# Four chained pairs of Strassen block products in place of eight plain up tiles, with sixteen modulation dots moved ahead of them

## The reference, cut to what matters

```python
h = modulate(rmsnorm(x, norm2_g[l]), sh2, sc2)
x = x + g2[:, None, :] * (jnp.square(jax.nn.relu(h @ w_up[l])) @ w_down[l])
shf, scf = jnp.split(c_act @ w_ada_final + b_ada_final, 2, axis=-1)
return modulate(rmsnorm(x, final_g), shf, scf)
```

## Time and profile before

| | us |
|---|---|
| median of 3 runs | 1181.98 |
| lowest, highest | 1180.6, 1182.74 |
| the profiled execution | 1180.96 |
| its span, first to last instruction | 1179.3 |
| PE busy | 1143.8 |
| DVE busy | 778.9 |
| ACT busy | 413.6 |

### The profile page before, as it was taken

The page is one execution under the profiler, slowest core; times in us unless marked ns, Lnnn a source line. Parts: engine busy times, 40 slices in busy tenths (PEclk is TensorE's granted clock), DMA queues, the critical chain, the costliest instruction groups (busy, mean ns, idle before and its releaser), DMA issues.

```text
span 1179.3 us, 17099 instructions
## 1 busy us (share of the span) xinstructions
PE 1143.8 (97%) x6522; PEld 1061.9 (90%) x6522; DVE 778.9 (66%) x1342; ACT 413.6 (35%) x683; POOL 76.9 (7%) x111
## 2 busy tenths in 40 slices
PE   6899999999999999999999999999999999999997
PEld 3786678888999999999889999999999999999886
DVE  6667898777645754565536677685756666457884
ACT  5521134454621211332316422253443525123324
POOL 3001110000111210000000000000000000000000
PEclk9899999999999999999999999999999999999998
DMA  9924553222252222275222241212221224223533
GB/s 354 361 71 161 168 203 131 80 74 71 82 179 99 98 99 98 97 278 160 91 72 108 90 138 58 71 58 68 72 67 59 72 73 142 72 89 117 166 91 108
DMA packets 45315, 139.96 MB, mean 119 GB/s; under 512 B 4876, under 2 KB 10588, under 8 KB 44093
## 3 DMA queue, kind: packets, MB, share of 16 engines
q1 hardware_dynamic: 28848, 81.36, 20.8%
q0 software_dynamic: 11344, 44.83, 11.0%
q10 hardware_dynamic: 5052, 12.81, 3.2%
HBM read 123.25 MB, written 15.74 MB: 118 GB/s over the span
## 4 chain that ended last, share of the span: by engine, by line
PE 92%; DVE 4%; issue 1%; ACT 1%; DMA 1%; SPq 0%; DVEq 0%; ACTq 0%
PE acc_ps L677 44%; PE acc_ps L1124 11%; PE acc_ps L755 11%; PE wk L1103 10%; PE wk L976 3%; PE wk L802 2%; PE wk L954 2%; PE acc_ps L762 1%; PE wk L895 1%; PE wk L916 1%; PE wk L905 1%; PE wk L795 1%; DMA xT_in<-in_x_T 1%; PE wk L868 0%; PE wk L929 0%
## 5 line engine op out<-in xcount | busy, mean ns | idle before, releaser
L677 PE MATMUL acc_ps<-act_hilo,w_hi 128*128 128x384 f32 x1792 | 398.1, 343 | 6.1 <-DVE act_hilo L1633 3.0
L677 PEld LDWEIGHTS acc_ps<-act_hilo,w_hi 128*128 128x128 f32 x1792 | 317.8, 190 | 26.6 <-issue 23.5
L677 PE MATMUL acc_ps<-act_hilo,w_lo 128*128 128x384 f32 x896 | 229.2, 336 | 0.0
L677 PEld LDWEIGHTS acc_ps<-act_hilo,w_lo 128*128 128x128 f32 x896 | 163.5, 190 | 0.0
L1587 DVE TENSOR_TENSOR w_lo<-w_raw,w_hi 128x1024 fp32r<-128x1024 f32 x70 | 85.5, 1222 | 91.9 <-ACT w_hi L1172 90.9
L1124 PE MATMUL acc_ps<-hid_st,w_st_hilo 128*128 128x384 f32 x768 | 134.3, 335 | 0.0
L1124 PEld LDWEIGHTS acc_ps<-hid_st,w_st_hilo 128*128 128x128 f32 x768 | 133.0, 188 | 0.7 <-issue 0.7
L1172 ACT ACTIVATE w_hi<-w_raw 128x1024 fp32r<-128x1024 f32 x70 | 73.7, 1053 | 95.3 <-PE acc_ps L677 87.9
L2116 DVE SCALAR_TENSOR_TENSOR xT<-acc_ps,modT,xT 128x384 f32<-128x384 f32 (+2 forms) x96 | 40.6, 479 | 58.9 <-PE acc_ps L1124 58.9
L2031 DVE CUSTOM_DVE_ANT_0 dot_out<-dot_ring,c_rows 128x1024 f32<-128x1024 f32 x48 | 58.8, 1224 | 5.1 <-DVE hidden_hilo L2047 4.3
L1678 DVE CUSTOM_DVE_ANT_0 dot_out<-dot_ring,c_rows,vecT 128x1024 f32<-128x1024 f32 x48 | 61.5, 1281 | 0.9
(11 more groups left out here) (259 smaller groups left out, 1861.6 us busy)
## 6 DMA issues: line engine op xcount, KB each, us to landing
w_raw<-in_w_pre SPq DMA_DIRECT2D x50, 512.0 KB, 3.5
dot_ring<-in_w_ada_cols POOLq DMA_DIRECT2D x48, 512.0 KB, 3.9
w_raw<-in_w_up SPq DMA_DIRECT2D x32, 512.0 KB, 3.5
w_raw<-in_w_down SPq DMA_DIRECT2D x16, 512.0 KB, 4.0
w_raw<-in_w_down_half SPq DMA_DIRECT2D x32, 256.0 KB, 2.6
spec<-filt_out POOLq DMA_DIRECT2D x12, 512.0 KB, 3.2
gate_spill<-gates_out ACTq DMA_DIRECT2D x16, 384.0 KB, 2.3
hy_spec<-spec SPq DMA_DIRECT2D x12, 512.0 KB, 5.5
```

The lines of the kernel that those rows point to most:

```text
L677: mm = pe.matmul(acc_ps[:, slot, 512 * h:512 * h + HALF], w[:, kw, :], src[:, x, k, HALF * h:HALF * h + HALF], start=(first and i == 0), s ...
```

## The change

- `NCH` and the second plain `up` go. The eight up tiles behind the groups become pairs 8 to 11 (`NPAIR` is 12), one behind another with no down tiles between them. Pairs 8, 9 and 10 use on ACT and DVE the list of an even pair (now a function `pair_ahead`), which prepares the next pair's operands; pair 11 ends with the splits of the first two tiles of the last down part among its own steps. The last down part reads its eight hidden blocks with the last two exchanged (0 to 5, 7, 6).
- Sixteen of the 24 late dots move from `up(1)` and the last down part into the four groups, four in each: behind combine 1 of the odd pair, behind the first down low part of the odd pair, and behind the residuals of down tiles 1 and 3. They use one row buffer, `ring3`, in place of two: POOL loads the next row when both sums of the dot before are done.
- The three late weight operands of a pair lie in a part of the activations that is free by then; the hidden blocks lie in `hid`; the sum of operand 6 shares its buffer with that of operand 1. Nothing else of the arithmetic changes.

The diff, cut to its core:

```diff
-            up_weights(1, first=1)
-            down_weights(1)
+            for q in range(2 * NHC, NPAIR):
+                pair_weights(q)
+            for m in range(KD):
+                if m < 2:
+                    pair_used(NPAIR - 1, m)
+                else:
+                    sp.wait_ge(hi_done, T_MLP + 16 + m - 1)
+                    sp.wait_ge(lo_done, T_MLP + 16 + m - 1)
+                sp.dma_start(raw[m % 2][:], w_down[KD + m]).then_inc(landed[m % 2], 16)
...
-            pool.wait_ge(st_mm, 7 * 2 * NHC)
-            pool.dma_start(cb2[:]...).then_inc(ld_c, 16)
-            late_loads(KD, DOTS - DOTS_OUT)
+            pool.wait_ge(acc_ready, A_MLP + 16)
+            pool.dma_start(cb3[:]...).then_inc(ld_c, 16)
+            for n in range(KD, DOTS - DOTS_OUT):
+                pool.wait_ge(dot_done, 2 * DOTS_OUT + 2 * n)
+                pool.dma_start(ring3[:], w_adaT[n + DOTS_OUT]).then_inc(ld_dot[2], 16)
...
-            pe.wait_ge(sd_free, KD * NHC)
-            up(NCH - 1)
+            for q in range(2 * NHC, NPAIR):
+                for j in range(7):
+                    product(q, j)
...
+            def spare_dot(n):
+
+                if n == KD:
+                    dve.wait_ge(ld_c, 48)
+                dve.wait_ge(ld_dot[2], 16 * len([i for i in range(DOTS_OUT) if i % 3 == 2]) + 16 * (n - KD + 1))
+                dve.wait_ge(late_done, n + 1)
+                for g in range(2):
+                    dve.wait_ge(dot_done, 2 * DOTS_OUT + g + 2 * n)
+                    dve.tensor_tensor_reduce(junk3[:], ring3[:], cb3[:, g], 1.0, 0.0, ALU.mult, ALU.add,
+                                             dacc[:, g:g + 1]).then_inc(dot_done, 1)
+                dve.wait_ge(dot_done, 2 * DOTS_OUT + 2 + 2 * n)
+                mt = n + DOT0 + DOTS_OUT
+                dve.tensor_scalar(modT[:, mt, :], dacc[:], vT[:, V_BA + mt:V_BA + mt + 1], None, ALU.add).then_inc(late_done, 1)
...
                 combine_st(q, 0)
                 combine_st(q, 1)
+                spare_dot(KD + 4 * hc)
                 combine_st(q, 2)
                 hidden_low(q, 0)
                 combine_st(q, 3)
                 combine_st(q, 4)
                 down_low(hc, 0)
+                spare_dot(KD + 4 * hc + 1)
                 combine_st(q, 5)
                 hidden_low(q, 1)
                 combine_st(q, 6)
...
                     if m + 3 < KD:
                         down_low(hc, m + 3)
+                    if m in (1, 3):
+                        spare_dot(KD + 4 * hc + 2 + m // 2)
...
-            dve.wait_ge(ld_c, 48)
-            up(NCH - 1, dots=KD)
+            dve.wait_ge(late_done, DOTS - DOTS_OUT + 1)
+            norm_scale(2)
+            for q in range(2 * NHC, NPAIR - 1):
+                pair_ahead(q)
+            q = NPAIR - 1
+            hidden_low(q - 1, 3)
+            op_low(q, 6)
+            combine_st(q, 0)
+            combine_st(q, 1)
+            combine_st(q, 2)
+            hidden_low(q, 0)
+            split_w(T_MLP + 16, 0, 16 * (landed_base + 9))
+            combine_st(q, 3)
+            combine_st(q, 4)
+            combine_st(q, 5)
+            hidden_low(q, 1)
+            split_w(T_MLP + 17, 1, 16 * (landed_base + 9))
+            combine_st(q, 6)
+            hidden_low(q, 2)
+            hidden_low(q, 3)
...
-                if u < KD:
-                    late_dot(2 * KD, u // 2, u % 2)
                 if u == KD:
-                    dve.wait_ge(late_done, DOTS - DOTS_OUT + 1)
-                    norm_scale(2)
                     norm_rstd(2, 0)
```

More of the change, by code:

```diff
@@ L433, in hid_block, with behind_pair @@
         def hid_block(q, b, x):
-            return hid4[:, x, 2 * (q % 2) + C_AT[b][0], HALF * C_AT[b][1]:HALF * C_AT[b][1] + HALF]
+            k = 2 * (q % 2) + C_AT[b][0] + (4 if q >= NPAIR - 2 else 0)
+            return hid[:, x, k, HALF * C_AT[b][1]:HALF * C_AT[b][1] + HALF]
+        def behind_pair(q):
+            return q % 2 == 1 or q == NPAIR - 2
         block = ctx.enter_context(nc.Block())
@@ L1140, in _ @@
                 if not h:
[L1141 removed]
+                    t = T_MLP + 16 + u
                     pe.wait_ge(hi_done, t + 1)
                     pe.wait_ge(lo_done, t + 1)
[L1144 to L1151, removed]
+                if u < 2:
+                    pe.wait_ge(sd_free, KD * NHC - 1 + u)
+                else:
+                    pe.wait_ge(acc_free[s], A_MLP // 2 + KD + u // 2)
+                for n in range(KD):
+                    k = n if n < KD - 2 else 2 * KD - 3 - n
+                    if u == 0 and n in (0, KD - 2, KD - 1):
+                        need = 4 * (NPAIR - 1) + {0: 0, KD - 2: 3, KD - 1: 4}[n]
+                        pe.wait_ge(h4_hi, need)
+                        pe.wait_ge(h4_lo, need)
+                    mm = group_k(s, w_last(m), h, k, hid, n)
+                    if n == KD - 1:
                         mm.then_inc(acc_ready, 1)
[L1153 removed]
+                    norm_first(2, u, n)
             norm_sum(2, 1)
@@ L2387, in laid_out @@
     down = np.asarray(inputs["w_down"])[0]
-    h["w_down"] = np.concatenate([tiles(down[D * i:D * i + D]) for i in range(NCH)])
-    h["w_down_half"] = np.concatenate([tiles(w) for w in down[D * NCH:].reshape(NHC, PK * P, D)])
+    h["w_down"] = np.concatenate([tiles(down[:D]), tiles(down[DFF - D:])])
+    h["w_down_half"] = np.concatenate([tiles(w) for w in down[D:DFF - D].reshape(NHC, PK * P, D)])
     return {n: np.ascontiguousarray(v) for n, v in h.items()}
```

182 lines of the change are left out of this document (103 added, 79 removed).

## The result

The changed kernel took 1188.08 us (median of 7 runs, 1186.54 to 1193.92) against 1180.6 us for the kernel before on the same chip (median of 7 runs, 1175.38 to 1182.74). The ratio, of the means, is 1.0078, 95% interval 1.0057 to 1.0098: slower by 9.2 us (6.7 to 11.6). A later repetition of both kernels gave 1.0055 (1.0037 to 1.0073), 6.5 us (4.4 to 8.6). The profiled execution of after took 1191.14 us, 1189.5 of them its span.

The account below looks back on a forecast made before the run. PE, holding 92% of the chain, was taken to bound the kernel. Savings -14.6, waits +13.2, clock +4.8 and pairs +0.3 made +3.7 us on 1180.96: 1184.7, as a median 1185.7 us, range 1175 to 1191.

Parts of the forecast that it names:

- The second dot's waits: Odd pair of each group: second dot waits for its row, combine 5 is late, PE waits 3.3 us; 13.2 us altogether.
- with its row in time: Rival: odd pair's second dot finds its row loaded; PE waits 1.9 us a group, clock holds, 1175.3 us; chance 0.10.
- The room of 0.27 us: Odd pair: combine 5 could be 0.27 us late before PE's fourth block in the first down tile waits.
- moved transfers: nothing: Pair 0: POOL's loads of c rows and first dot row fall beside pair 1's weights, with 3 us room; no cost.
- The clock behind the waits: Each group's first down tile: granted clock falls after PE's idle times, costing 1.2 us a group, 4.8 us altogether.
- the bound of 1.74: Groups: slow clock behind the waits costs between 0 and 1.74 us each, the upper figure taken from `up(1)`.
- Fewer matmuls and the start of the stage: Up tiles behind the groups: 336 matmuls for 384 save 8.32 us; no idle PE or slow clock at start saves 3.48.
- The last norm and the first tile: Last part: norm wait falls from 1.84 to 0.73 us, 2.8 saved with the clock; first down tile's 0.86 wait stays.
- The dots behind down tiles: Groups: dots behind down tiles 1 and 3 cost nothing, since the next tile takes back some 0.3 us.
- The chain of pairs: Pairs 8 to 11: operands fall 0.5 us further behind per pair, still in time; 0.3 us taken, at most 1.1.
- The rival in which the chain falls behind: Pairs 9 to 11: with slower landings operands miss their time, some 4 us more, 1189.7 us; chance 0.15.
- The sum: Whole kernel: savings of 14.6 us against 13.2, 4.8 and 0.3 us added, giving +3.7 us.

Follow-up runs that it names:

- fifth experiment: Kernel with the second dot moved and c rows loaded later, plus two unread 512-column additions on DVE ahead of combine 5 in each odd pair: 1168.5 us (one run).
- first and fourth experiments: First: changed kernel, odd pair's second dot moved behind a residual, 1168.01 us. Fourth: that kernel, with loads of c rows and first dot row held back, 1166.71 us.

## Why the prediction was right, and where it was off

The forecast was 1185.7 us in a range of 1175 to 1191; 1188.08 came. Direction and mechanism were right, the size was not: the change was forecast at +3.7 us, and the timings give +9.2 and +6.5. That the time itself came so near is in part luck, since the kernel before ran 1.4 us faster beside it than the 1181.98 that the forecast was built on. By its steps:

*The second dot's waits: right in cause, too small in size, 16.0 us for 13.2.* The steps are there: idle 1.39 us before the dot (1.4), combine 5 3.6 to 3.7 us late (3.57) in groups 1 to 3. Moving this one dot removed 21.1 us, and with its row in time the cost was 2.1 to 2.7 us (1.9). Two things are missing in the 13.2.

The room of 0.27 us was not there. It was the 870.43 worked out for PE's fourth block less the 870.16 at which hidden_low 3 ends. But the block starts at 870.31 in that trace, and PE doesn't start when DVE ends: in the rows above hidden_low 3 ends at 1019.08 + 0.56 = 1019.64 and PE starts at 1019.78, 0.14 us later. The fifth experiment has the room at 0.02 to 0.07 us. That is 0.2 us in each group.

Group 0 waits longer. Its cause was costed at nothing ("moved transfers: nothing"). The loads of the c rows and of the first dot row delay pair 1's weights by more than their room, and the first sum comes 1.4 us late. Nothing of that is caught up: combine 5 is 5.2 us late for 3.6 to 3.7 in the others, and the fourth block 5.16. With the loads later the first sum was on time and the last 0.46 us of wait went. The idle times, 13.3 us for 13.2, agree with the prediction only by luck: they leave out 0.16 us per wait and all of group 0's second one.

*The clock behind the waits: nearly right, 5.7 us for 4.8* (4.9 in the repetition). Filling the waits shows that it is the clock, with 5.2 us in three groups. Per group it was 0.5, 2.8, 0.9 and 1.5 us for the 1.2 I took, so the sum is in part luck; part of the slow stretch did fall into the second wait, most of all in group 0. Group 1 breaks the bound of 1.74, with the clock low in three pieces of 2 us in a row. The bound came from a stage with one wait and one slow stretch, and I took it for a limit. The prediction gave 7.0 us as the price by the Trainium skill (TensorE: Matmul & The Clock Gate, "HAM oscillation — how this bites in real kernels"), that the return to full clock is paid each time. The trace agrees that every one of the four groups paid, in both executions; what they paid, 5.7 and 4.9 us, is nearer to my 4.8.

*Fewer matmuls and the start of the stage: right*, 70.04 - 58.24 = 11.8 us. But the 1.74 us of slow clock within it are a saving only in executions in which the clock falls there; in the repeated kernel before it did not, and the saving would be 68.62 - 58.24 = 10.4.

*The last norm and the first tile.* The norm's wait is 0.72 us (0.73 predicted from its twin) at full clock; it gave some 2.6 us (2.8). The first tile of the last part lost its 0.86 us wait, which I had left standing: a gain of about 1 us.

*The dots behind down tiles: nothing, right*, also in three places instead of two.

*The chain of pairs: right.* DVE's first sums in after, pairs 8 to 10 (pair starts 1051.70, 1066.26, 1080.82):

```profile
1058.58 0.69 DVE L2106 TENSOR_TENSOR s_sum<-w_raw 128x512 f32<-128x512 f32 x1 [1.95 <-DMA w_raw<-in_w_up]
...
1073.64 0.69 DVE L2106 TENSOR_TENSOR s_sum<-w_raw 128x512 f32<-128x512 f32 x1 [0.95 <-DMA w_raw<-in_w_up]
...
1088.78 0.69 DVE L2106 TENSOR_TENSOR s_sum<-w_raw 128x512 f32<-128x512 f32 x1 [1.02 <-DMA w_raw<-in_w_up]
```

They come at +6.9, +7.4 and +8.0: a drift of 0.5 and 0.6 us a pair, as worked out, though in pairs 9 and 10 0.9 us sooner than I had put them, and no wait of PE. The rival in which the chain falls behind is out; the loop was not far from it, though: combine 1 ends 3.3 us behind the first sum, at +11.3 in pair 10 where +12.5 is the limit, so two or three more pairs would have used that up.

*The sum.* Off by 2.8 (waits) + 0.9 (clock) - 1.0 (last part, the first tile above all) - 0.3 (pairs) - 0.1 (end) = +2.3 us on +3.7, which is the +6.0 of the stages. That lies in the interval of the second timing (+4.4 to +8.6 us) and 0.7 us under that of the first (+6.7 to +11.6).

Left open: what sets how much the slow clock costs behind a wait, between 0.9 and 2.8 us in groups with nearly equal waits, and whether the dots alone could have been moved in the kernel before. The latter wasn't tried; the c rows now lie in the space that `hid_st` has in the kernel before. Nor were the c rows and the first dot row held back one without the other.

The first and fourth experiments show a version faster than both kernels: 1166.71 us, 1.2% under before, by the places of one dot and one load.

## What to carry to other kernels

Work moved onto an engine that runs a fixed list needs room at that point of the list, not idle share: the same 2.67 us dot cost nothing behind a residual and 21.1/4 = 5.3 us between two steps whose result PE was waiting for. With one buffer, two consumers on the list must stand a reload apart (0.3 + 3.6 to 3.9 us after the first one's last read), and the wait between them holds up everything queued behind. A wait put into a loop is to be priced with the slow clock behind it, here about 0.3 us for each 1 us of delay, and the delay is to be read from starts, not from idle time. Room between two engines is counted with the hand-over between them, here 0.14 us.

## What the runs showed of the hardware that was not expected

- The same 1.74 us of idle PE, at the same place of the same kernel, was followed by 0.50 granted clock in one execution and 1.00 in another.
- In groups with a fourth block nearly equally late (3.55 to 3.64 us) the slow clock cost 0.9, 1.5 and 2.8 us; pairs of waits of 0.96 to 1.63 and some 0.75 us left the clock at 1.00 in three groups of three.
- At full clock a group grew by combine 5's delay less 0.02 to 0.07 us, in eleven groups of four kernels; PE's idle time shows 0.16 us less per wait.
- A load of 1 MB by POOL, with one of 512 KB behind it, held the first use of a weight tile loaded by SP back by some 1.4 us.
- Identical code ahead of pair 0 took 772.1 to 779.9 us in profiled executions, as much as the whole effect of the change.
